# Moving the row-maximum pieces and the row broadcast of a windowed attention stage to other steps of the TensorE order

## The reference, cut to what matters

```python
# latent queries, for each block of 128 queries; band = 128 + 2 * 128 keys
s_loc = where(|i - j| <= 128, q @ k_band.T * scale, -inf)
s_ctx = q @ k_ctx.T * scale                      # 256 context keys
s_sink = sink[head]
p = softmax(concat([s_loc, s_ctx, s_sink]))
o = p[:band] @ v_band + p[band:band + 256] @ v_ctx
```

## Time and profile before

| | |
|---|---|
| time, median of 3 | 1714.55 us (1714.26 to 1717.87) |
| the profiled execution | 1717.87 us, span 1716.1 us |
| PE busy | 1594.8 us (93%) |
| DVE, ACT, POOL busy | 886.6, 565.8, 583.8 us |
| layer 1's attention | 1156.9 to 1280.1 us of the span |
| layer 0's attention | about 247 to 345 us of the span |

### The profile page before, as it was taken

How to read it: one execution, slowest core, us unless ns; L and a number is a source line. 1 busy time by engine, 2 the same in 40 slices (tenths; PEclk the granted TensorE clock), 3 DMA queues, 4 the chain that set the end, 5 groups by cost and what they waited for, 6 DMA issues and landing times.

```text
span 1716.1 us, 25160 instructions
## 1 busy us (share of the span) xinstructions
PE 1594.8 (93%) x10716; PEld 1318.6 (77%) x10716; DVE 886.6 (52%) x1253; ACT 565.8 (33%) x729; POOL 583.8 (34%) x259
## 2 busy tenths in 40 slices
PE   6698978774899999999999999999999999999997
PEld 3677864334688888888888888885558998998995
DVE  4698745546335787656556634366654231221224
ACT  4644553330533221122212223325544322232232
POOL 1145213440122233233222332325563444444432
PEclk9899987885899999999999999999999999999998
DMA  8433310000312333333343322220002232223222
GB/s 331 152 113 133 108 52 0 1 2 3 123 62 99 123 123 124 125 127 129 135 143 127 124 74 74 74 63 1 1 1 98 87 99 86 99 87 111 87 98 98
DMA packets 41631, 158.61 MB, mean 92 GB/s; under 512 B 4624, under 2 KB 5008, under 8 KB 39728
## 3 DMA queue, kind: packets, MB, share of 16 engines
q1 hardware_dynamic: 41232, 156.74, 26.5%
q0 software_dynamic: 288, 0.26, 0.1%
HBM read 154.89 MB, written 2.10 MB: 91 GB/s over the span
## 4 chain that ended last, share of the span: by engine, by line
PE 83%; DVE 10%; issue 3%; ACT 1%; POOL 1%; DMA 1%; SPq 0%; DVEq 0%; ACTq 0%; POOLq 0%
PE psum L1576 68%; PE psum L1734 2%; DVE mx L1124 2%; PE psum L1655 1%; PE psum L1704 1%; PE psum L1749 1%; POOL acc L558 1%; DVE product L994 1%; PE psum L1596 1%; DMA ada_w<-ada_dram 1%; PE psum L1721 1%; PE psum L1706 1%; PE psum L1676 1%; PE psum L1708 1%; PE psum L1710 1%
## 5 line engine op out<-in xcount | busy, mean ns | idle before, releaser
L1576 PE MATMUL psum<-act,whi 128*128 128x512 f32 (+1 forms) x4064 | 808.0, 319 | 6.1 <-DVE bsm L1043 3.6
L584 POOL TENSOR_TENSOR wlo<-raw,whi 128x1024 fp32r<-128x1024 f32 (+1 forms) x181 | 437.7, 2418 | 975.1 <-ACT whi L607 975.1
L1576 PEld LDWEIGHTS psum<-act,whi 128*128 128x128 f32 x4064 | 605.6, 190 | 66.8 <-issue 7.6
L1576 PE MATMUL psum<-act,wlo 128*128 128x512 f32 (+1 forms) x2032 | 485.5, 317 | 0.0
L1576 PEld LDWEIGHTS psum<-act,wlo 128*128 128x128 f32 x2032 | 317.5, 190 | 28.0
L994 DVE SCALAR_TENSOR_TENSOR product<-adr,cb 128x1024 f32<-128x1024 f32 x128 | 269.1, 2132 | 128.0 <-DMA adr<-adat_dram 127.4
L607 ACT ACTIVATE whi<-raw 128x1024 fp32r<-128x1024 f32 (+1 forms) x181 | 188.1, 1039 | 317.4 <-DMA raw<-weights_dram 317.2
L1042 DVE SCALAR_TENSOR_TENSOR tmps<-psum,rs 128x256 f32<-128x256 f32 (+1 forms) x176 | 78.0, 484 | 201.8 <-PE psum L1576 197.8
L1576 PE MATMUL psum<-gh,whi 128*128 128x512 f32 (+1 forms) x528 | 160.8, 358 | 0.0
L1576 PE MATMUL psum<-gh,wlo 128*128 128x512 f32 (+1 forms) x528 | 160.7, 359 | 0.0
L1576 PE MATMUL psum<-gl,whi 128*128 128x512 f32 (+1 forms) x528 | 159.2, 355 | 0.0
(11 more groups left out here) (182 smaller groups left out, 1267.8 us busy)
## 6 DMA issues: line engine op xcount, KB each, us to landing
raw<-weights_dram SPq DMA_DIRECT2D x181, 512.0 KB, 3.5
adr<-adat_dram SPq DMA_DIRECT2D x80, 512.0 KB, 4.5
ada_w<-ada_dram SPq DMA_DIRECT2D x8, 1024.0 KB, 15.2
xT<-x_in_dram SPq DMA_DIRECT2D x4, 1536.0 KB, 13.0
cb<-crow_dram SPq DMA_DIRECT2D x2, 1024.0 KB, 8.2
out_dram<-big SPq DMA_DIRECT2D x8, 256.0 KB, 2.2
con<-consts_dram SPq DMA_DIRECT2D x1, 512.0 KB, 7.3
con<-consts_dram SPq DMA_DIRECT2D x1, 320.0 KB, 3.3
```

What stands on the lines that cost most here:

```text
L584: nc.gpsimd.tensor_tensor(wlo[:, s, 0:w], raw[:, s, 0:w], whi[:, s, 0:w].bitcast(F32), ALU.subtract).then_inc(sem("s_lo"), 1)
L1576: last = MM(out_[:, o:o + t1 - t0], w_, a_[:, t0:t1], start=k == order[0] and j == 0, stop=k == order[-1] and j == 2)
```

## The change

In layer 1 alone, the pieces, the row broadcast and `out_low` stand at other steps:

```diff
 def pieces_beside(layer, i, a):
 
     units = UNITS[layer]
-    if layer == 1:
-        n, p = (i + 1, 4) if a == 0 else (i + 2, a - 2)
-        return [], [(n, p)] if n < len(units) and p >= 0 else []
+    if layer == 1 and i == 0:
+        return {0: ([], [(1, 4)]), 1: ([], []), 2: ([], [(2, 0)]), 3: ([(2, 1)], [(2, 2)]), 4: ([(2, 3)], [(2, 4)]),
+                5: ([], [])}[a]
     if layer == 0 and i == 0 and a == 0:
         return [(1, 4)], [(1, 5)]
     if a == 0 or a == 5 or i + 2 >= len(units):
...
+    if len(units[n]["pieces"]) == 5:
+        return {1: ([], [(n, 0)]), 2: ([], [(n, 1)]), 3: ([(n, 2)], [(n, 3)]), 4: ([], [(n, 4)])}[a]
     return [], [(n, a - 1)]
 
 
 def rows_at(layer, i):
 
-    return layer
+    return 1 if layer == 1 and i == 0 else 0
...
-                        if a == (4 if L == 1 or not short else 1) and i >= 1:
+                        if a == (1 if short else 4) and i >= 1:
                             out_high(i - 1)
...
-                        if a == (1 if short else 5 - L) and i >= 1:
+                        if a == (1 if short else 5) and i >= 1:
                             out_low(i - 1)
```

## The result

The changed kernel took 1739.26 us, median of 4 runs (1733.68 to 1741.74), beside 1716.21 for the kernel before: a ratio of 1.0125 (95% interval 1.0109 to 1.0141). A second set gave 1735.93 and a ratio of 1.0122 (1.0102 to 1.0142). It is slower, by 21 us; 18.5 were forecast. The time of 1739 us lies inside the stated range (1720 to 1745) and 1 us above the narrower band of the forecast itself (1729 to 1738).

The account below looks back on a forecast made before the run. PE's own list was taken to bound layer 1's attention. Waits of 3.3 us a unit, 16.5 for units 1 to 5, plus 2.0 for unit 0 gave +18.5 us: 1733 us on the median, forecast 1729 to 1738, range 1720 to 1745.

Parts of the forecast that it names:

- PE's own work: Layer 1's attention: PE issues the same instructions, so its work changes by 0, with 0.2 us a unit either way.
- B: Units 1 to 5, step 3: PE's piece 3, behind `scores`, waits 0.30 us for the reduction of piece 2.
- A: Units 1 to 5, step 3: PE's piece 2, ahead of `scores`, waits 0.80 us for the reduction of piece 1.
- C: Units 1 to 5: `values` of step 5 waits 0.5 us for its exponential, late because POOL's add slows `outputs`.
- D: Units 1 to 5: the next unit's first `values` waits 1.7 us for the evacuation, bounds 0.5 and 2.8.
- Unit 0: Two pieces in steps 3 and 4: waits for reductions 1.7 us, masked pieces that stand alone 0.3, together 2.0.
- The two old waits: PE's 1.9 us for `top` of unit 1 and 1.4 us before the last `sums`, both forecast to stay.
- rival 2: Layer 1's attention: more blocking by `q_low` (1740 us), or the clock falls behind waits (1743 to 1750); chance 0.22.
- its other half: `q_low` meets POOL's add of step 3, piece 2's reduction comes 1.4 us later: +7, 1740 us; chance 0.08.

Follow-up runs that it names:

- e3: Changed kernel with POOL's adds of steps 4 and 5 in layer 1 cut to 8 columns; 1725.82 us, ratio 1.0057.
- e5: Changed kernel with the reductions of the pieces of units 2 to 7 reading only the first half of each query's keys; 1722.56 us, ratio 1.0036.
- e6: Kernel before with the double step alone: pieces 1 and 2 in step 3, piece 3 in step 4; 1725.70 us, ratio 1.0049.
- e1: Changed kernel with `out_low` of layer 1 moved behind the evacuation; 1734.04 us, ratio 1.0095.
- e2: Changed kernel with `evacuate` first, then `top` and `out_low` behind it; 1727.44 us, ratio 1.0057.
- e9: Kernel before with POOL's first add of unit 0 waiting for `top` of unit 1; 1714.24 us, ratio 0.9986.
- e7: Kernel before with the row broadcast alone moved from step 1 to step 0 for units 1 and up; 1724.74 us, ratio 1.0047.
- e8: Changed kernel with no double step in units 1 to 5: pieces 0 to 4 in steps 1 to 5, one each; 1731.34 us, ratio 1.0091.
- e4: Kernel before with POOL's adds of steps 4 and 5 in layer 1 cut to 8 columns, as control; ratio 0.9994.

## Why the prediction was right

It was right in sign, in size and in mechanism, but one term that it priced at nothing was 3 us, and it was lucky in that its errors cancel. The trace without a fall of the clock allows the sum to be checked. The stage grew by 141.99 - 123.22 = 18.8 us against 18.5. PE's waits grew by 15.8 of them: 7.1 for reductions, 7.3 for the evacuation, 1.4 for the exponential. PE's own busy time grew by 122.90 - 119.92 = 3.0.

- **PE's own work, costed at 0, give or take 0.2 a unit: the one term that was wrong in kind.** PE is busy 16.0 a unit against 15.63, 0.37 more. Piece 2 alone with its mask took 0.80, as the 0.79 that I read for it. What I left out is that a wait also lengthens the work ahead of it: without one, the next group of matmuls starts while this one is ending. The last matmuls of `scores` ahead of wait B took their whole 0.34, where before the change the next group started 0.18 behind them, and `values` ahead of wait A took 0.65 instead of 0.58. Two experiments issue the changed kernel's instructions on PE in the same order and wait less, one unit of e3 and one of e5:

```profile
1184.95:1201.88 16.93, 15.86 (x112) 8.83 (x111) 9.56 (x12) 8.36 (x12) 6.08 (x5) 1.00 0.01 2
1213.65:1229.88 16.23, 15.78 (x111) 8.84 (x111) 8.23 (x12) 8.38 (x12) 9.23 (x5) 1.00 0.00 0
```

  PE is busy 15.86 without C and D, and 15.78 without B and C. So at least 0.2 of the 0.37 comes and goes with the waits; how the rest is shared between the waits and the new order is not shown. The same holds for the 0.35 of e6, which has two waits a unit.
- **A, 0.80**: 0.83. **B, 0.30**: 0.24. Both are the reduction's length less what PE has in hand; by shortening it e5 brought A to 0.3 and B to nothing.
- **C, 0.5**: 0.28. The add took 1.82, less than the 2.08 I used, and PE came 0.1 later than I had it. e3 shows that it comes from the add.
- **D, 1.7**: 1.45. Its four terms in the trace: reduction 1.21, `top` 1.95, `out_low` and `evacuate` 0.68 each. e1 shortened it, and e2 and e3 took it away, from different sides.
- **Unit 0, 2.0**: about 2.9. Its waits are 0.39, 0.51, 0.34 and 0.47, the 1.7 that were forecast; the rest, 1.2, is PE's own time, which I had priced at 0.3. Two masked pieces stand alone there instead of one, and the four waits lengthen what is ahead of them (0.86 instead of 0.79 for one `values`); the two are not separated.
- **Moving `out_low` from step 4 to step 5 does nothing by itself.** I listed it as part of the arrangement, and did not see that with the pieces moved DVE has nothing between the two places: `taken` with `top` comes ahead of both. e1 shows what a place behind the evacuation is worth, 0.6 us a unit.
- **The two old waits** stayed, as forecast, at 1.9 and 1.4.

Per unit the errors nearly cancel: 3.3 forecast, 3.18 measured, of which 2.8 are waits. The waits were forecast 0.5 too long and PE's own work 0.37 too short. That the sum of the stage came out to 0.3 us is luck in this sense.

The times are 2 to 3 us further apart than these stages. That is within their noise: the lower ends of the two intervals are 18.7 and 17.5 us. The clock, one half of rival 2, can have a share: it fell twice, for 1.8 us, in one trace of two, which is the sign that the prediction named for being wrong (PEclk below 1.00). The spread of the times doesn't show it: 21 runs of the changed kernel are 8.1 us apart and 21 of the kernel before 7.5. How often the clock falls in an average run was not counted. The 1743 to 1750 us of this rival did not come. Nor did its other half: `q_low` started at 1203.01, 0.28 us ahead of the add of step 3, and took 0.68.

## What to carry to other kernels

An engine with a third of its time free can still be what another waits for at one place. Read how long after its release each result is wanted, and add up what is queued ahead of it on its engine: two such sums, for the double step and for the unit's tail, gave this result to half a microsecond a unit. Where two engines slow each other, the order in which they start decides, and it can turn on 0.2 us: here a reduction shorter by half gave back the waits behind a different instruction. Where the busy time of the bound engine grows although it does the same work, look at the waits: part of what each costs stands in the busy time ahead of it. And a part of the same program that already has the proposed arrangement (here layer 0) shows before a run which waits will come, if not how long they are: its waits for the evacuation are 2.5 us on average, those of the change 1.45.

## What the runs showed of the hardware that was not expected

The wait for `top` in unit 0 is 1.9 us long in every kernel that has it. In the traces of e1 to e5 the clock fell to 0.50 about when it ended (from 0.3 us ahead of its end to 1.8 us behind) and stayed there for 7 to 10 us (4 to 9 is what I wrote ahead of e9, too little); in the traces of before, e6, e7 and e8 and in both of the changed kernel it stayed at 1.00. This is the control with short adds (e4), in four windows from the wait on:

```profile
1160.00:1164.00 4.00, 2.08 (x14) 1.75 (x14) 2.08 (x2) 0.60 (x1) 1.66 (x2) 0.82 0.00 0
1164.00:1168.00 4.00, 4.00 (x22) 2.80 (x20) 1.82 (x2) 1.42 (x2) 1.46 (x1) 0.50 0.00 0
1168.00:1172.00 4.00, 4.00 (x28) 2.73 (x26) 1.23 (x1) 0.87 (x2) 0.67 (x2) 0.83 0.00 0
1172.00:1176.00 4.00, 4.00 (x28) 2.25 (x28) 2.20 (x3) 1.56 (x2) 0.22 (x1) 1.00 0.01 4
```

Nor does it take a long wait. The clock fell five more times in this stage: twice behind an evacuation wait (1.45 in the changed kernel, 1.80 in e8), and three times 0.4 to 0.5 us behind the pair of waits A and B of the double step, 0.83 and 0.24, in the changed kernel, e1 and e3. In e3, for instance, wait B ended at 1227.40, and the masks at 1227.77 took 0.79 instead of 0.50. Most waits of the same lengths had no such sequel.

So one trace with the clock at 1.00 behind a wait, as the earlier trace rows has it, says nothing about the next run: the prediction used it as evidence that 1.9 us are harmless, and they are not. Of two executions of one kernel, as the two traces of the changed kernel show, one may pay for a wait twice, once for its length and once at 1.2 GHz behind it. For the wait in unit 0 it is five traces of eleven, but of ten kernels: whether the kernel, the chip or chance decides there is not shown. The Trainium skill ("TensorE: Matmul & The Clock Gate", section "What's actually happening") has the number of slow matmuls at the start of a kernel differ between runs of it. What differs here is in the middle of a kernel, and it is the same kind of thing.
